# A decoder trunk on one core: score products moved ahead of a branch block, and the opening's first weights split in three pieces on another queue

## The reference, cut to what matters

```python
h = rms_norm(x, norm_mix[layer])
proj = h @ w_in                        # all head groups of four mixers, and four gates
o_a = sliding_window_attention(...)    # 8 heads of 64, window 128, learned sinks
o_b = dsa_attention(...)               # 8 heads, 64 chosen keys per query
o_c = retention(...)                   # 4 heads
o_d = multiscale_pool(...)
up = einsum("btnc,ncd->btnd", stack(o_a, o_b, o_c, o_d), w_branch)
x = x + sum(sigmoid(gates) * up) @ w_out
x = x + memory_cross_attention(rms_norm(x), rms_norm(mem))
x = x + (swiglu(rms_norm(x)) if layer == 0 else moe_ffn(rms_norm(x)))
```

## Time and the profile before

| what | before |
|---|---|
| median of 3 runs | 1901.4 us (1901.31 to 1901.84) |
| the profiled execution, its own time | 1902.32 us |
| its span, first to last instruction | 1900.5 us |
| PE busy | 1882.9 us (99%) |
| VectorE busy | 790.1 us (42%) |
| ScalarE busy | 571.2 us (30%) |
| mean granted TensorE clock | 0.998 |

### The profile page before, as it was taken

The page is one execution under the profiler, slowest core; times in us unless marked ns, Lnnn a source line. Parts: engine busy times, 40 slices in busy tenths (PEclk is TensorE's granted clock), DMA queues, the critical chain, the costliest instruction groups (busy, mean ns, idle before and its releaser), DMA issues.

```text
span 1900.5 us, 31300 instructions
## 1 busy us (share of the span) xinstructions
PE 1882.9 (99%) x13904; PEld 1138.7 (60%) x13904; DVE 790.1 (42%) x1076; ACT 571.2 (30%) x766; POOL 100.7 (5%) x188
## 2 busy tenths in 40 slices
PE   8999999999999999999999999999999999999998
PEld 7887888888888888788884333333333333333343
DVE  6877767656555677766844110101010010101013
ACT  6566554554444546654542000000000000000001
POOL 4300000000000030001000100000000000000100
PEclk9999999999999999999999999999999999999999
DMA  8445555455555544567558999999999999999994
GB/s 290 161 142 174 157 187 187 134 182 194 181 195 175 190 157 154 155 177 253 180 213 298 415 417 419 420 418 419 420 420 419 420 416 417 417 414 421 407 417 185
DMA packets 157256, 542.62 MB, mean 286 GB/s; under 512 B 11416, under 2 KB 35552, under 8 KB 128448
## 3 DMA queue, kind: packets, MB, share of 16 engines
q1 hardware_dynamic: 153120, 529.39, 74.2%
q0 software_dynamic: 3472, 10.91, 1.5%
q10 hardware_dynamic: 528, 0.29, 0.1%
HBM read 531.11 MB, written 9.45 MB: 284 GB/s over the span
## 4 chain that ended last, share of the span: by engine, by line
PE 98%; DVE 1%; ACT 0%; issue 0%; DMA 0%; SPq 0%; DVEq 0%; ACTq 0%
PE bank L2738 30%; PE bank L2280 14%; PE bank L2281 14%; PE bank L2282 14%; PE bank L2752 10%; PE bank L2762 5%; PE bank L2672 3%; PE bank L2328 2%; PE bank L2670 2%; PE bank L2346 1%; PE bank L2368 1%; PE bank L2696 0%; DVE low_in_place L1407 0%; PE bank L2795 0%; PE bank L2477 0%
## 5 line engine op out<-in xcount | busy, mean ns | idle before, releaser
L2738 PE MATMUL bank<-ring,o_buf 128*32 128x512 f32 (+1 forms) x6144 | 581.1, 539 | 0.5 <-issue 0.3
L2280 PE MATMUL bank<-w_hi,stat 128*128 128x512 f32 (+1 forms) x1168 | 458.5, 393 | 0.5 <-DVE low_in_place L2215 0.5
L2281 PE MATMUL bank<-low_in_place,stat 128*128 128x512 f32 (+1 forms) x1168 | 453.4, 388 | 0.0
L2282 PE MATMUL bank<-w_hi,stat 128*128 128x512 f32 (+1 forms) x1168 | 453.3, 388 | 0.0
L2738 PEld LDWEIGHTS bank<-ring,o_buf 128*32 128x32 f32 x6144 | 205.9, 110 | 374.4 <-issue 361.4
L1407 DVE TENSOR_TENSOR low_in_place<-raw,w_hi 128x2048 fp32r<-128x2048 f32 (+1 forms) x161 | 367.2, 2283 | 137.9 <-ACT w_hi L933 137.5
L933 ACT ACTIVATE w_hi<-raw 128x2048 fp32r<-128x2048 f32 (+1 forms) x161 | 305.7, 1904 | 219.2 <-DMA raw<-in_dense_w_gu 59.5
L2280 PEld LDWEIGHTS bank<-w_hi,stat 128*128 128x128 f32 x1168 | 219.9, 188 | 50.1 <-issue 6.1
L2282 PEld LDWEIGHTS bank<-w_hi,stat 128*128 128x128 f32 x1168 | 219.9, 188 | 45.2
L2281 PEld LDWEIGHTS bank<-low_in_place,stat 128*128 128x128 f32 x1168 | 220.1, 188 | 42.7
L1970 DVE TENSOR_TENSOR area<-bank,area 128x512 f32<-128x512 f32 (+1 forms) x48 | 30.4, 688 | 508.1 <-PE bank L2738 508.1
(11 more groups left out here) (354 smaller groups left out, 1203.7 us busy)
## 6 DMA issues: line engine op xcount, KB each, us to landing
ring<-in_moe_w_gu SPq DMA_DIRECT2D x128, 1024.0 KB, 15.9
ring<-in_moe_w_gu SPq DMA_DIRECT2D x128, 768.0 KB, 16.6
ring<-in_moe_w_down SPq DMA_DIRECT2D x64, 1024.0 KB, 16.3
raw<-in_w_in SPq DMA_DIRECT2D x55, 1024.0 KB, 5.0
ring<-in_moe_w_down SPq DMA_DIRECT2D x32, 1536.0 KB
raw<-in_dense_w_gu SPq DMA_DIRECT2D x28, 1024.0 KB, 5.1
raw<-in_w_xkv SPq DMA_DIRECT2D x16, 1024.0 KB, 5.3
raw<-in_dense_w_down SPq DMA_DIRECT2D x14, 1024.0 KB, 5.0
```

What stands on the lines that cost most here:

```text
L2280: pe.matmul(dst, x_hi, wh, start=start, stop=False)
L2281: pe.matmul(dst, x_hi, wl, start=False, stop=False)
L2282: return pe.matmul(dst, x_lo, wh, start=False, stop=stop)
L2738: ins = pe.matmul(dsts[g][rows_of(j), 0:n], x_t[:, g, k, :], w[:, j, :, :], start=(k == 0), stop=(k == KD - 1))
```

## The change: what it does

`scores_of(layer, "a1")` is called behind block (gateD0, 1), right after `outs_of(layer, "a0")`, where it was called behind block (upD0, 0). The order of `small_uses`, and DVE's and ACT's streams around it, stay. It holds in both layers.

In the opening, the first block's weights go to ACT's queue in three pieces (weight tile 0, tile 1, tiles 2 and 3); SP's queue now begins with x's first quarter, then gains, x's second quarter, block 1, x's second half, block 2, and takes over the four small gain loads and the positions ahead of block 3. ACT rounds weight tile 0 before it splits h0, DVE makes its remainder before it splits h0. PE does six float32 128 x 128 products of the identity (`warm_up`) before the gain transpose and three behind the transposes of h0; block (pu, 0) goes by weight tile, both token tiles for each, and h2 and h3 are transposed behind it.

```diff
@@ -388,7 +388,7 @@
         gains_landed = sem("gains_landed")
         more_landed = sem("more_landed")
         pos_landed = sem("pos_landed")
-        first_landed = sem("first_landed")
+        first_landed = [sem(f"first_landed{kt}") for kt in range(2)]
         first_hi = sem("first_hi")
         first_lo = sem("first_lo")
         mem_landed = sem("mem_landed")
@@ -711,20 +711,20 @@
                 else:
                     load_block((0, n), chunk_source(c.name, i, layer), c.n)
 
+            def load_x(part, first, last):
+
+                start(x[:, :, first:last], x_in[0, :, first:last].rearrange("(t p) d -> p t d", p=P), x_landed[part])
+
+            load_x(0, 0, 256)
             start(gain_rows[:, :], norm_mix.rearrange("l (k p) -> (l k) p", p=P), gains_landed)
-            first_block = chunk_source("pu", 0, 0)
-
-            def load_x(part, first, last):
-
-                start(x[:, :, first:last], x_in[0, :, first:last].rearrange("(t p) d -> p t d", p=P), x_landed[part])
-
-            load_x(0, 0, 256)
-            start(raw[:, 0, 0:2, :], first_block[:, 0:2, :], first_landed)
             load_x(1, 256, 512)
-            start(raw[:, 0, 2:4, :], first_block[:, 2:4, :], raw_landed[0])
+            load_planned(1)
             load_x(2, 512, 1024)
-            load_planned(1)
             load_planned(2)
+            for row, src, n in ((0, norm_cross, 16), (16, norm_mem, 16), (32, norm_ffn, 16), (48, pool_scale, 8)):
+                start(more_rows[row:row + n, :], src.rearrange("l (k p) -> (l k) p", p=P), more_landed)
+            sp.dma_start(pos_i[:, :], positions[0].rearrange("(t p) -> p t", p=P),
+                         allow_slow_non_contiguous=True).then_inc(pos_landed, 16)
             load_planned(3)
             load_planned(4)
             start(tok[:, :, :], mem_in[0].rearrange("(t p) d -> p t d", p=P), mem_landed)
@@ -1323,20 +1323,19 @@
 
             def first_block_hi(kt):
 
-                if kt % 2 == 0:
-                    act.wait_ge(raw_landed[0] if kt else first_landed, 16)
+                if kt < 3:
+                    act.wait_ge(raw_landed[0] if kt == 2 else first_landed[kt], 16)
                 act.wait_ge(block_used, 1)
                 act.activation(w_hi[:, 0, kt, :], raw[:, 0, kt, :], ACT.Copy).then_inc(hi_done if kt == 3 else first_hi, 1)
 
-            act.dma_start(pos_i[:, :], positions[0].rearrange("(t p) -> p t", p=P),
-                          allow_slow_non_contiguous=True).then_inc(pos_landed, 16)
-            for row, src, n in ((0, norm_cross, 16), (16, norm_mem, 16), (32, norm_ffn, 16), (48, pool_scale, 8)):
-                act.dma_start(more_rows[row:row + n, :], src.rearrange("l (k p) -> (l k) p", p=P)).then_inc(more_landed, 16)
+            first_block = chunk_source("pu", 0, 0)
+            for n, (lo_kt, hi_kt) in enumerate(((0, 1), (1, 2), (2, 4))):
+                act.dma_start(raw[:, 0, lo_kt:hi_kt, :], first_block[:, lo_kt:hi_kt, :]).then_inc(raw_landed[0] if n == 2 else first_landed[n], 16)
             act.wait_ge(consts_ready, 1)
             act.activation(rrt[:, 0, 0:1], eps_sb[:, :], ACT.Copy)
+            first_block_hi(0)
             act.wait_ge(setup_free, 1)
             split_gain(0, "h0", stat0, "mix", 0)
-            first_block_hi(0)
             first_block_hi(1)
             split_gain(0, "h1", stat0, "mix", 1)
             first_block_hi(2)
@@ -2209,11 +2208,13 @@
             dve.tensor_copy(gains[:, 0:16], bank[0][:, 0:16]).then_inc(setup_free, 1)
             dve.wait_ge(setup_free, 1)
             for kt in range(4):
-                if kt % 2 == 0:
-                    split_gain(0, f"h{kt // 2}", stat0, "mix", kt // 2)
+                if kt == 2:
+                    split_gain(0, "h1", stat0, "mix", 1)
                 dve.wait_ge(hi_done if kt == 3 else first_hi, 1 if kt == 3 else kt + 1)
                 ins = dve.tensor_tensor(low_in_place[:, 0, kt, :], raw[:, 0, kt, :], f32_of(w_hi[:, 0, kt, :]), ALU.subtract)
                 ins.then_inc(lo_done if kt == 3 else first_lo, 1)
+                if kt == 0:
+                    split_gain(0, "h0", stat0, "mix", 0)
             lo_planned(1)
             split_gain(0, "h2", stat0, "mix", 2)
             split_gain(0, "h3", stat0, "mix", 3)
@@ -2283,15 +2284,20 @@
 
             def consume(b, stationary, k0, dsts, n, first, last, low=in_place_lo, between=None, signal_rows=False):
 
-                opening = number(b) == 0
-                if not opening:
-                    pe.wait_ge(lo_done, number(b) + (1 + SLOTS))
+                if number(b) == 0:
+                    for kt in range(4):
+                        opening_piece(kt)
+                        for t, dst in enumerate(dsts):
+                            ins = product(dst[:, 0:n], stationary, k0 + kt, slice(t * P, (t + 1) * P), b, low(b), kt, n,
+                                          first and kt == 0, last and kt == 3)
+                    ins.then_inc(block_used, 1)
+                    between()
+                    return
+                pe.wait_ge(lo_done, number(b) + (1 + SLOTS))
                 for t, dst in enumerate(dsts):
                     if t and between is not None:
                         between()
                     for kt in range(4):
-                        if opening and t == 0:
-                            opening_piece(kt)
                         ins = product(dst[:, 0:n], stationary, k0 + kt, slice(t * P, (t + 1) * P), b, low(b), kt, n,
                                       first and kt == 0, last and kt == 3)
                     if t == 0 and signal_rows:
@@ -2306,6 +2312,11 @@
                     pe.wait_ge(first_lo, kt + 1)
                 else:
                     pe.wait_ge(lo_done, 1 + SLOTS)
+
+            def warm_up(n):
+
+                for i in range(n):
+                    pe.matmul(bank[3][:, 0:P], ident[:, :], ident[:, :], start=True, stop=True)
 
             def opened(layer, name):
 
@@ -2554,7 +2565,6 @@
                     retention_outs(layer)
                 elif at == ("gateD0", 1):
                     outs_of(layer, "a0")
-                elif at == ("upD0", 0):
                     scores_of(layer, "a1")
                 elif at == ("upD1", 0):
                     probs_of(layer, "a1")
@@ -2836,11 +2846,14 @@
 
             pe.sem_inc(block_used, SLOTS)
             pe.wait_ge(consts_ready, 1)
+            warm_up(6)
             pe.wait_ge(gains_landed, 16)
             pe.transpose(bank[0][:, 0:16], gain_rows, ident[0:16, 0:16]).then_inc(setup_full, 1)
             for q in range(2):
                 pe.wait_ge(x_landed[q], 16)
                 rows_t(0, f"h{q}", x, q)
+                if q == 0:
+                    warm_up(3)
             pe.wait_ge(setup_free, 1)
 
             for layer in range(DEPTH):
```

More of the change, by code:

```diff
@@ L712, in load_planned @@
                     load_block((0, n), chunk_source(c.name, i, layer), c.n)
-            start(gain_rows[:, :], norm_mix.rearrange("l (k p) -> (l k) p", p=P), gains_landed)
-            first_block = chunk_source("pu", 0, 0)
             def load_x(part, first, last):
@@ L721, in _ @@
             load_x(0, 0, 256)
-            start(raw[:, 0, 0:2, :], first_block[:, 0:2, :], first_landed)
+            start(gain_rows[:, :], norm_mix.rearrange("l (k p) -> (l k) p", p=P), gains_landed)
             load_x(1, 256, 512)
-            start(raw[:, 0, 2:4, :], first_block[:, 2:4, :], raw_landed[0])
+            load_planned(1)
             load_x(2, 512, 1024)
-            load_planned(1)
             load_planned(2)
+            for row, src, n in ((0, norm_cross, 16), (16, norm_mem, 16), (32, norm_ffn, 16), (48, pool_scale, 8)):
+                start(more_rows[row:row + n, :], src.rearrange("l (k p) -> (l k) p", p=P), more_landed)
+            sp.dma_start(pos_i[:, :], positions[0].rearrange("(t p) -> p t", p=P),
+                         allow_slow_non_contiguous=True).then_inc(pos_landed, 16)
             load_planned(3)
```

## The result

The changed kernel takes 1920.97 us (median of 5 runs, 1920.03 to 1921.41) against 1901.4 us, a ratio of 1.0102, 95% interval [1.0091, 1.0114]: 19.6 us slower, where 13.6 were predicted (1915.0, range 1911.5 to 1918.5). The profiled execution took 1921.41 us with a span of 1919.6 us; the mean granted clock of TensorE is 0.994, against 0.998 before. A line of before is one less in the new file for DVE (L1664 is L1663), eleven more for PE's small products (L2346 is L2357, L2328 is L2339).

The account below looks back on a forecast made before the run. PE, holding 98% of the chain, was taken to bound the kernel. 1902.32 - 0.5 (opening) + 11.3 (bank stalls) + 2.6 (late softmax) = 1915.7, 1914.8 in medians, written as 1915.0 us; range 1911.5 to 1918.5.

Parts of the forecast that it names:

- The sign: Whole kernel: slower with probability 0.96, same 0.03, faster 0.01.
- The two bank waits: At the moved scores, PE waits about 2.7 and 2.85 us for banks; stalls of 5.66 and 5.64 us, together 11.3.
- DVE's copy that does not move: In layer 0, DVE's copy of a0's outputs stays at 132.82 to 133.51 us, holding the second pair of scores.
- the softmax that is late behind the gating: At a1's transposed probabilities, PE waits 1.3 us per layer, 2.6 in both, because DVE gates upD0 before the mask.
- the sum of the two stalls: Bank stall before upD0 plus the wait at a1's transposed probabilities, 6.95 us per layer.
- the first rival: Behind the score gaps the clock drops, 12 products go at 0.427 us, 2.3 us more per layer: 1919.6 us; 13%.
- The opening: Start of the kernel, up to block (pu, 1): a gain of 0.5 us, bounds 1.4 gained to 1.3 lost.
- The wait for (pu, 1): In the opening, PE is through at about 19.7 us and waits for DVE's remainder; (pu, 1) starts at 21.2.
- the bounds of 8.2 and 8.6: In the opening, limits in us for the start of PE's first product, taken at 8.4.
- The count of slow products: In the opening, 4 products at the slow clock level instead of 12, bounds 0 and 12.

Follow-up runs that it names:

- e3: Changed kernel with eleven extra products of 512 columns on PE ahead of each pair of moved scores, computing nothing of the result; 1916.58 us.
- e2: Kernel before with only the second group's scores moved, its opening kept; 1920.95 us, ratio 1.0105 to before.
- e4: Changed kernel with DVE copying a0's outputs right behind the retention outputs, ahead of the remainder; 1915.67 us.
- e5: Changed kernel with DVE putting the mask and maximum of a1's scores ahead of the gating of upD0; 1918.41 us.
- e6: Changed kernel with both DVE edits, a0's copy ahead of the remainder and the mask ahead of the gating; 1911.79 us.
- the eight executions named above: Profiled executions with the changed opening: the changed kernel and seven follow-up runs; a0's outputs started between 124.38 and 126.53 us.
- e7: Changed opening without its nine float32 identity products, scores at their old place; 1903.09 us, ratio 1.0012 to the kernel before.
- e9: The kernel before, unchanged, profiled a second time; 1900.81 us in one run.
- e8: Changed opening with h2 and h3 transposed between weight tiles 1 and 2 of (pu, 0), scores at their old place; 1900.90 us.
- e12: Changed kernel with DVE's bank-freeing work and the mask earlier, h2 and h3 transposed inside (pu, 0); 1900.47 us against 1901.55 for before.

## Why the prediction was wrong

- **The sign and the main mechanism: right.** The two bank waits, DVE's copy that does not move, and the softmax that is late behind the gating came as worked out. With the clock held (e3) the sum of the two stalls is 7.03 us per layer against 6.95 predicted, and the time 1916.6.
- **The failed step: the clock.** The prediction counted on products 0.23 us apart behind the gaps and gave the first rival, the fall of the clock, 13%. It happened in both layers of the changed kernel and of e2, e4, e5 and e6. The arguments against it (1.06 us of work between the gaps, dense work on both sides) had no row behind them. The Trainium skill, TensorE: Matmul & The Clock Gate, Why this matters for your kernels, advises against idle gaps between bursts of matmuls because the clock drops to its lower level; the trace agrees on the drop, with 0.50 behind a gap of 2.82 us, but this gap is somewhat shorter than those that the section warns of, and the measurement decides.
- **The rival was also priced too low**, at 2.3 us a layer for 12 slow products. Measured is 9.73 - 7.03 = 2.7 and 9.90 - 7.07 = 2.8. It has two parts. The scores are slow too: each pair takes 1.0 us more. The first pair's surplus is free, since the second pair waits for the copy anyway (its wait shrinks from 2.85 to 1.75); the second pair's is on the path, and upD0 starts 9.74 us behind the outputs instead of 8.78. Then eight or nine products of upD0 at 0.43 instead of 0.23 cost another 1.7 to 1.9. With that the rival's time would have been 1915 + 5.5 = 1920.5. The 0.5 us left to 1920.97 is as much as the opening was to gain and did not.
- **The mask behind the gating**: predicted 1.3 per layer, measured 1.44; e5 returned 2.6 us for both layers.
- **The opening**: predicted a gain of 0.5 us; alone it measured +0.06% [-0.03, +0.15], which can't be told from none and speaks for a small loss rather than a gain. The wait for (pu, 1) was right. PE's first product started at 8.05 in the changed kernel, below the bounds of 8.2 and 8.6, but between 8.03 and 9.03 over the eight executions named above; the prediction let x's landing set this start and left out the gains, which came 2.6 us later than before. The count of slow products was the wrong quantity to forecast: it changes between executions of one program. The Trainium skill says that too, in TensorE: Matmul & The Clock Gate, What's actually happening; here the old opening had 6 to 12 of them in three profiles, and the new one 0 to 6 in ten, 7 in e7 without the nine products.
- **Left open.** In layer 1, ahead of the second transposes of the cross attention, PE waits 0.7 us for DVE's residual (L1694, at 926.26 in the changed kernel). It is there in eight of eleven profiles with the new opening and in none of the three with the old one (before, e2, e9). It would take back part of what e8 and e12 gain at the start. What causes it was not tried.

## What to carry to other kernels

When work is moved forward on an engine, look up who must empty the buffers that it reuses and where that release stands in the other engine's order, and move the release with it: here three calls moved in VectorE's order, two of them into time in which it was idle, took the 19 us back, down to 0.04% [-0.06, +0.13] over the kernel before. Price a new gap in TensorE's work as the gap plus slow work behind it, 1.1 to 3.0 us for a gap of 2.8 us in this kernel, and count small products among the slow ones. An opening's gain of one or two microseconds needs many executions to be told from the scatter of the clock's rise.

## What the runs showed of the hardware

- The granted clock fell to 0.50 behind a single gap of 2.8 us, in the middle of a kernel that had kept TensorE busy for 100 us and more (e4, e6), and it fell at different places: within the gap in layer 0 of the changed kernel (0.90 at 126:128), and after the scores had begun again in layer 1 of e4 (the pair at 748.44 took 1.28 us, the next 2.08).
- Filling the gaps with products that compute nothing made the kernel 4.4 us faster (e3 against the changed kernel); the clock stayed at 1.00.
- In the opening the profile's clock column shows 1.00 while the products stand 0.43 us apart. There the distance between starts tells the level, not the column.
